# 56 unused floats between the activation buffers and the weight buffers of a hybrid encoder trunk

## The chip, the cores and the metric

The kernel runs on one core of one Trainium2 chip. The metric is the device time of one execution in microseconds (us), lower is better. Three timed runs of the kernel before gave 1882.45 us as median, from 1880.82 to 1882.71.

## The reference

Two layers of an encoder over 512 frames and 16 learned meta tokens, so 528 positions of width 1024. Every layer stands between two half-step SwiGLU feed-forward blocks. Layer 0 mixes with a gated convolution and a state space model, layer 1 with windowed attention; its second half keeps the 512 real positions only.

```
h = concatenate([meta, x])                      # 528 x 1024
for layer in range(2):
    h = h + 0.5 * (silu(n1(h) @ w_gate) * (n1(h) @ w_up)) @ w_down     # d_ff 2816
    mix = conv_ssm_mixer(nm(h)) if layer == 0 else window_attention(nm(h))
    h = h + mix                                 # layer 1: without the meta tokens
    h = h + 0.5 * (silu(n2(h) @ w_gate2) * (n2(h) @ w_up2)) @ w_down2
```

## The kernel before, in words

Everything is float32. TensorE multiplies in the float32r format, and to keep the precision each product is made of three: every weight block is split into a high part `wh` and a low part `wl`, every activation into `xh`, `xl` (or `act_h`, `act_l` behind the gate), and `mm3` (L790 to L801) adds wh*xh, wh*xl and wl*xh in PSUM.

The stationary operand (the one that LDWEIGHTS puts into the array) is a block of 128 columns of `wh` or `wl`; the moving operand is a row of an activation buffer, all positions of one group of 128 features. With 528 positions a row is streamed in two matmuls of 264 columns (`hf` 0 and 1, column description `ALL`), each with a weight load of its own; with 512 positions in one matmul of 512 (`FRONT`).

```
for q, (w, x) in enumerate(((wh, x_h), (wh, x_l), (wl, x_h))):
    for hf in range(nb):
        last = nc.tensor.matmul(ps[:, 2 * pair + hf, 0:nh], w[:, slot, b * P:(b + 1) * P],
                                x[:, k0 + k, c0 + hf * nh:c0 + (hf + 1) * nh], ...)
```

Feed-forward blocks 0 to 2 (`ffn`, through `x_job` and `mm3`, recorded at L799) run with 528 positions, block 3 with 512. L1015 is the input projection of layer 0, L1057 its output projection, L1076 keys and values of layer 1 (there the activations are stationary and the weights move), L1126 the queries, L1227 and L1265 the output projection of the attention.

**Where the operands lie.** Buffers stand one behind the other in each partition, in the order of their `sb` calls: `h`, `xh`, `xl`, `act_h`, `act_l`, `raw`, `wh`, `wl`, `t_a` and the smaller ones, `arena`. A row of the activations is padded from 528 to `ROW` = 576 floats, 2304 bytes, which is 9 times 256; a weight block is 512 bytes and all the large buffers are multiples of 256 bytes long. So an activation row and a weight block start at the same place modulo 256 (in the built program both at 128). From this follows the position of each moving operand relative to its stationary one, in bytes modulo 256:

- 528 positions: `hf` 0 at 0, `hf` 1 at 264 * 4 = 1056, which is +32
- 512 positions in block 3, L1227, L1265: 0 (in 48 of the 96 matmuls of L1265 the stationary operand, too, lies in the activation buffers, `w3h` and `w3l`)
- L1126 starts at position 16: +64
- L1076, where `xh` from position 16 on is stationary and the weights move: -64

The order of work is fixed. SP loads units of 16 weight blocks into the two slots of `raw` (`load_unit`, L699), each load waiting for the low part of an earlier unit (`wl_ready`); ScalarE copies `wh` from `raw` (L1276), VectorE subtracts to get `wl` (L1563), TensorE consumes the unit. ScalarE and VectorE also evaluate the gates, the norms and the residual (L1314 to L1316, L1599 to L1624) on tiles that `tile_full` announces.

Of the kernel before, what the change touches and what calls it, by code (L numbers as in the profile page):

```python
# [25 lines left out]
P = 128  # L26
# [6 lines left out]
def trunk_program(nc, a, out, stop=None):  # L33
# [56 lines left out]
    with ExitStack() as ctx:  # L90
        def sb(name, shape, dt=F32):
            return ctx.enter_context(nc.sbuf_tensor(name, shape, dt))
# [6 lines left out]
        xl = sb("xl", [P, KD, ROW], F32R)[:, :, 0:L]  # L99
        act_h = sb("act_h", [P, PART[0], ROW], F32R)[:, :, 0:L]  # L100
        act_l = sb("act_l", [P, PART[0], ROW], F32R)[:, :, 0:L]
        raw = sb("raw", [P, 2, UNITW])
        wh = sb("wh", [P, 2, UNITW], F32R)
        wl = sb("wl", [P, 2, UNITW], F32R)
# [1986 lines left out]
```

## Time and profile before

| | |
|---|---|
| timed, median of 3 | 1882.45 us |
| profiled execution, device time | 1882.0 us |
| its span, first to last instruction | 1880.0 us |
| TensorE matmuls / weight loads | 13887 / 13887 |
| granted TensorE clock, mean | 0.998 |

The profile gives for every engine its busy time, in groups of instructions by line, operation and operands. `PE` is a matmul, `PEld` a weight load. A matmul is pipelined: its duration in the trace runs from its start to the arrival of its last result, and the next one starts long before. What a matmul costs in a dense stretch is therefore the distance from one start to the next, which the timeline and the chain of work give, not the mean duration. The chain of work lists what the last instruction depended on, back to the beginning.

### The profile page before, as it was taken

The numbers are of one execution on the slowest core, as the hardware profiler recorded it, in microseconds if no ns is written. First come the engines' busy times: TensorE is split into PE (matmuls) and PEld (weight loads), VectorE is DVE, ScalarE is ACT, GpSimd is POOL, SyncE is SP. The second block draws the span as 40 slices with busy tenths as digits, with TensorE's granted clock in tenths as the row PEclk, the third lists the DMA queues.
The fourth block names the chain that finished last, engine by engine and source line by source line (L and its number), as shares of the span: only waits on it lengthen the run. The fifth ranks groups of instructions, "written<-read, shape, count | busy, mean of one in ns | idle before, by whom it ended". The sixth has DMA issues, their size and how long they took to land.

```text
span 1880.0 us, 33855 instructions
## 1 busy us (share of the span) xinstructions
PE 1865.3 (99%) x13887; PEld 1765.6 (94%) x13887; DVE 955.1 (51%) x1077; ACT 599.6 (32%) x707; POOL 350.8 (19%) x629
## 2 busy tenths in 40 slices
PE   8999999999999999999999999999999999999999
PEld 8999999999999999999999999999988788888887
DVE  5444356568765443344564443445556654434443
ACT  5222222332243222222342222223456442222232
POOL 2888889414330000000000000000012000000000
PEclk9999999999999999999999999999999999999999
DMA  7332444547523332433243323322321233333423
GB/s 183 90 84 84 142 147 128 163 126 185 137 69 90 90 84 84 120 82 83 70 126 90 84 84 101 90 81 71 112 73 46 62 96 92 92 94 104 110 70 87
DMA packets 330785, 188.29 MB, mean 100 GB/s; under 512 B 8152, under 2 KB 323832, under 8 KB 330712
## 3 DMA queue, kind: packets, MB, share of 16 engines
q1 hardware_dynamic: 323296, 166.81, 32.0%
q0 software_dynamic: 7088, 20.38, 4.0%
q8 instruction: 52, 0.85, 0.2%
q14 instruction: 21, 0.17, 0.0%
q10 hardware_dynamic: 328, 0.07, 0.0%
HBM read 174.91 MB, written 11.14 MB: 99 GB/s over the span
## 4 chain that ended last, share of the span: by engine, by line
PE 95%; DVE 2%; issue 1%; ACT 1%; DMA 1%; ACTq 0%; POOL 0%; SPq 0%; DVEq 0%
PE ps L799 78%; PE ps L1015 5%; PE ps L1057 2%; PE ps L1126 2%; PE ps L1076 1%; PE ps L1265 1%; PE ps L1227 1%; DMA raw<-in_ff_w_down 1%; PE ps L844 1%; PE ps L1167 0%; PE ps L976 0%; PE ps L975 0%; PE ps L966 0%; DVE r L1592 0%; DVE wl L1563 0%
## 5 line engine op out<-in xcount | busy, mean ns | idle before, releaser
L799 PE MATMUL ps<-xh,wh 128*128 128x264 f32 (+1 forms) x2432 | 557.7, 299 | 0.3 <-DVE t_a L1616 0.2
L799 PE MATMUL ps<-xh,wl 128*128 128x264 f32 (+1 forms) x2432 | 556.6, 298 | 0.0
L799 PE MATMUL ps<-xl,wh 128*128 128x264 f32 (+1 forms) x2432 | 556.6, 298 | 0.0
L1563 DVE TENSOR_TENSOR wl<-raw,wh 128x2048 fp32r<-128x2048 f32 x171 | 398.3, 2329 | 173.6 <-ACT wh L1276 173.6
L1276 ACT ACTIVATE wh<-raw 128x2048 fp32r<-128x2048 f32 x172 | 327.5, 1904 | 248.6 <-PE ps L799 205.7
L799 PEld LDWEIGHTS ps<-xh,wh 128*128 128x128 f32 x2432 | 384.9, 188 | 15.3 <-issue 1.4
L799 PEld LDWEIGHTS ps<-xl,wh 128*128 128x128 f32 x2432 | 384.8, 188 | 13.8 <-issue 0.2
L799 PEld LDWEIGHTS ps<-xh,wl 128*128 128x128 f32 x2432 | 384.8, 188 | 13.8
L799 PE MATMUL ps<-act_h,wh 128*128 128x264 f32 (+1 forms) x1232 | 282.2, 298 | 1.2 <-DVE wl L1563 1.2
L799 PE MATMUL ps<-act_h,wl 128*128 128x264 f32 (+1 forms) x1232 | 281.6, 298 | 0.0
L799 PE MATMUL ps<-act_l,wh 128*128 128x264 f32 (+1 forms) x1232 | 281.5, 298 | 0.0
L1619 DVE TENSOR_TENSOR t_c<-ps,r 128x528 f32<-128x528 f32 (+1 forms) x88 | 61.9, 704 | 358.3 <-PE ps L799 356.5
L799 PEld LDWEIGHTS ps<-act_h,wh 128*128 128x128 f32 x1232 | 194.8, 188 | 8.2 <-issue 1.4
L799 PEld LDWEIGHTS ps<-act_h,wl 128*128 128x128 f32 x1232 | 194.8, 188 | 7.0
L799 PEld LDWEIGHTS ps<-act_l,wh 128*128 128x128 f32 x1232 | 194.9, 188 | 6.6
L1316 ACT ACTIVATE act_h<-t_c 128x528 f32 (+3 forms) x88 | 56.5, 642 | 447.8 <-DVE t_c L1622 447.8
L326 POOL TENSOR_TENSOR arena<-arena 128x32 f32<-128x32 f32 (+6 forms) x253 | 183.1, 724 | 19.6
L676 POOL TENSOR_SCALAR arena<-arena 128x16 f32<-128x16 f32 x4 | 1.0, 258 | 871.6 <-DVE arena L1948 842.3
L1314 ACT ACTIVATE t_bs<-t_a 128x528 f32<-128x528 f32 (+1 forms) x88 | 56.5, 643 | 274.6 <-DVE t_a L1616 274.6
L1599 DVE SCALAR_TENSOR_TENSOR h<-ps,h 128x528 f32 (+2 forms) x72 | 50.6, 703 | 182.0 <-PE ps L799 174.9
L1624 DVE TENSOR_TENSOR act_l<-t_c,act_h 128x528 f32 (+3 forms) x88 | 65.8, 747 | 78.5 <-ACT act_h L1316 78.5
L1622 DVE TENSOR_TENSOR t_c<-t_c,t_bs 128x528 f32<-128x528 f32 (+1 forms) x88 | 68.0, 773 | 9.0
(308 smaller groups left out, 1681.3 us busy)
## 6 DMA issues: line engine op xcount, KB each, us to landing
raw<-in_ff_w_gate SPq DMA_DIRECT2D x88, 512.0 KB, 4.0
raw<-in_ff_w_up SPq DMA_DIRECT2D x87, 512.0 KB, 5.2
raw<-in_ff_w_down SPq DMA_DIRECT2D x64, 384.0 KB, 4.0
raw<-in_ff_w_down SPq DMA_DIRECT2D x64, 320.0 KB, 3.7
raw<-in_even_w_in SPq DMA_DIRECT2D x16, 512.0 KB, 5.3
raw<-in_attn_w_qkv SPq DMA_DIRECT2D x12, 512.0 KB, 4.4
raw<-in_even_w_out SPq DMA_DIRECT2D x8, 512.0 KB, 4.5
raw<-in_attn_w_o SPq DMA_DIRECT2D x8, 512.0 KB, 4.6
```

Source lines behind the costliest of these rows:

```text
L326: did(g.tensor_tensor(o, x, y, op))
L799: last = nc.tensor.matmul(ps[:, 2 * pair + hf, 0:nh], w[:, slot, b * P:(b + 1) * P], x[:, k0 + k, c0 + hf * nh:c0 + (hf + 1) * nh], start= ...
L1015: last = nc.tensor.matmul(ps[:, 2 * (p % 2) + hf, 0:L // 2], w[:, slot, b * P:(b + 1) * P], x[:, k, hf * L // 2:(hf + 1) * L // 2], start= ...
L1057: last = nc.tensor.matmul(ps[:, 2 * (d % 2) + hf, 0:L // 2], w[:, slot, b * P:(b + 1) * P], x[:, k, hf * L // 2:(hf + 1) * L // 2], start= ...
L1276: nc.scalar.activation(wh[:, c % 2, :], raw[:, c % 2, :], ACT.Copy).then_inc(wh_ready, 1)
L1314: nc.scalar.activation(t_b[:, cols], t_a[:, cols], ACT.Silu).then_inc(silu_done[n], 1)
L1316: nc.scalar.activation(act_h[:, s + 2 * i, span(operand(col))], t_c[:, cols], ACT.Copy).then_inc(act_h_done[n], 1)
L1563: v.tensor_tensor(wl[:, c % 2, :], raw[:, c % 2, :], wh[:, c % 2, :].bitcast(F32), ALU.subtract).then_inc(wl_ready, 1)
L1599: v.scalar_tensor_tensor(hd, tile(pair, col), scale, hd, ALU.mult, ALU.add).then_inc(tile_evac, 1)
L1619: v.tensor_tensor(halves(t_c, col), tile(1, col), halves(r, col), ALU.mult).then_inc(tile_evac, 1)
L1622: v.tensor_tensor(t_c[:, cols], t_c[:, cols], t_b[:, cols], ALU.mult).then_inc(gated[n], 1)
L1624: v.tensor_tensor(act_l[:, s + 2 * i, span(operand(col))], t_c[:, cols], act_h[:, s + 2 * i, span(operand(col))].bitcast(F32), ALU.subtrac ...
```

## The change

One buffer of 56 floats (224 bytes) per partition is allocated between `act_l` and `raw`. Nothing reads or writes it. `raw`, `wh`, `wl` and everything allocated after them move up by 224 bytes; `h`, `xh`, `xl`, `act_h`, `act_l` stay. No instruction is added, removed or reordered.

```
         act_h = sb("act_h", [P, PART[0], ROW], F32R)[:, :, 0:L]
         act_l = sb("act_l", [P, PART[0], ROW], F32R)[:, :, 0:L]
+        weight_pad = sb("weight_pad", [P, 56])
         raw = sb("raw", [P, 2, UNITW])
         wh = sb("wh", [P, 2, UNITW], F32R)
         wl = sb("wl", [P, 2, UNITW], F32R)
```

Relative to its stationary operand, modulo 256 bytes, each moving operand goes 32 bytes up: 528 positions from 0 and +32 to +32 and +64; 512 positions from 0 to +32; L1126 from +64 to +96; L1076, where the weights move, from -64 to -96. The 48 matmuls of L1265 with both operands in the activation buffers stay at 0.

## Rows read from the trace of the kernel before

**Rows 1.** The page: busy time of the engines, and granted clock in 40 slices

```profile
PE 1865.3 (99%) x13887; PEld 1765.6 (94%) x13887; DVE 955.1 (51%) x1077; ACT 599.6 (32%) x707; POOL 350.8 (19%) x629
...
PEclk9999999999999999999999999999999999999999
```

**Rows 2.** The chain of work, pieces in order: start us, us, what

```profile
43.73 299.54 PE ps L799 x2496
...
593.92 374.64 PE ps L799 x3120
...
975.25 368.88 PE ps L799 x3072
...
1523.87 307.64 PE ps L799 x1356
```

**Rows 3.** Waits of TensorE: waited for, us in total, times, longest

```profile
PE ps L916 <- DMA arena<-in_meta_tokens: 3.0, 1, 3.0
...
PE ps L799 <- DVE wl L1563: 1.2, 1, 1.2
```

**Rows 4.** Waits of the SP queue

```profile
SPq L703 <- DVE wl L1563: 1515.4, 167, 21.7
```

**Rows 5.** Groups by line and shape on TensorE: xcount, busy us, mean ns

```profile
L799 PE MATMUL ps<-xh,wh 128*128 128x264 f32 x2080 | 420.3, 283 | 0.1
...
L799 PE MATMUL ps<-act_h,wh 128*128 128x264 f32 x1056 | 213.1, 283 | 1.2 <-DVE wl L1563 1.2
...
L799 PE MATMUL ps<-xh,wh 128*128 128x512 f32 x352 | 137.5, 391 | 0.2 <-DVE t_a L1616 0.2
...
L799 PE MATMUL ps<-act_h,wh 128*128 128x512 f32 x176 | 69.1, 393 | 0.0
...
L1015 PE MATMUL ps<-xh,wh 128*128 128x264 f32 x256 | 53.3, 290 | 0.5 <-DVE arena L1751 0.5
...
L1126 PE MATMUL ps<-xh,wh 128*128 128x512 f32 x64 | 26.6, 415 | 0.0
L1057 PE MATMUL ps<-act_h,wh 128*128 128x264 f32 x128 | 25.8, 284 | 0.3 <-DVE act_l L1854 0.3
...
L1227 PE MATMUL ps<-act_h,wh 128*128 128x512 f32 x32 | 14.0, 436 | 0.0
L1076 PE MATMUL ps<-wh,xh 128*128 128x512 f32 x32 | 12.9, 402 | 0.0
...
L1265 PE MATMUL ps<-act_h,wh 128*128 128x512 f32 x16 | 6.2, 389 | 0.0
```

**Rows 6.** Weight loads of L799, the same columns

```profile
L799 PEld LDWEIGHTS ps<-xh,wh 128*128 128x128 f32 x2432 | 384.9, 188 | 15.3 <-issue 1.4
```

**Rows 7.** Timeline of TensorE in the first matmuls: start us, us, what

```profile
17.77 0.65 PE L844 MATMUL ps<-xh,wh 128*128 128x264 f32 x2
...
20.41 0.65 PE L844 MATMUL ps<-xh,wh 128*128 128x264 f32 x2
```

**Rows 8.** Timeline of TensorE in block 3, two matmuls, thirty-nine apart

```profile
1700.11 0.39 PE L799 MATMUL ps<-act_h,wh 128*128 128x512 f32 x1
...
1708.95 0.39 PE L799 MATMUL ps<-xh,wh 128*128 128x512 f32 x1
```

**Rows 9.** Timeline of TensorE in the queries, L1126, thirty-nine matmuls apart

```profile
1371.23 0.39 PE L1126 MATMUL ps<-xh,wh 128*128 128x512 f32 x1
...
1380.16 0.39 PE L1126 MATMUL ps<-xh,wh 128*128 128x512 f32 x1
```

**Rows 10.** Timeline of TensorE in keys and values, L1076, forty matmuls apart

```profile
1360.05 0.39 PE L1076 MATMUL ps<-wh,xh 128*128 128x512 f32 x1
...
1369.38 0.39 PE L1076 MATMUL ps<-wh,xl 128*128 128x512 f32 x1
```

**Rows 11.** Windows: busy (instructions) of PE, PEld, DVE, ACT, POOL; clock, DMA share, GB/s

```profile
0.00:40.00 40.00, 33.28 (x224) 32.28 (x225) 22.43 (x31) 23.40 (x35) 10.25 (x22) 0.91 0.77 197
40.00:400.00 360.00, 358.77 (x2989) 358.41 (x2988) 176.97 (x153) 101.35 (x91) 263.16 (x422) 1.00 0.41 119
...
550.00:1345.00 795.00, 794.93 (x6612) 794.14 (x6611) 369.20 (x342) 233.59 (x215) 6.81 (x13) 1.00 0.32 90
```

More of the change, by code:

```diff
@@ L101, in trunk_program @@
         act_l = sb("act_l", [P, PART[0], ROW], F32R)[:, :, 0:L]
+        weight_pad = sb("weight_pad", [P, 56])
         raw = sb("raw", [P, 2, UNITW])
```

## The prediction

> **What bounds the kernel now.** I read the page first. TensorE is busy for 99% of the span and has as many weight loads as matmuls; VectorE and ScalarE are half idle or more, and the clock is full in all forty slices [rows 1]. A busy TensorE can still be a waiting one, so the waits come next: the longest of TensorE is 3.0 us for the first input, and all waits for a weight unit in L799 together are 1.2 us [rows 3]. SP, which loads the weights, is ahead: it stands for 1515 us waiting for a slot to come free [rows 4]. The chain of work says the same: long pieces in which nothing but matmul follows matmul [rows 2]. So the time is the number of matmuls times the distance between two starts, and that distance is the only thing that an unused buffer can move.
>
> The distances. With 264 columns: 374.64 us for 3120 matmuls is 120.1 ns, 299.54 for 2496 is 120.0, 368.88 for 3072 is 120.1 [rows 2]. At 2.4 GHz and one column a cycle the columns alone are 110.0 ns, so 10.0 ns are on top. With 512 columns in block 3: from 1700.11 to 1708.95 are 39 matmuls, 226.7 ns each [rows 8]; columns alone 213.3, on top 13.3. In the first matmuls, at the low clock, 12 matmuls take 2.64 us, 220.0 ns each [rows 7], and 264 columns at 1.2 GHz are 220.0: nothing on top. So the extra belongs to the full clock and is no fixed price of an instruction. Every matmul has the load of the next weights beside it, which the trace shows with 188 ns from start to end whatever the matmul's length [rows 6]. A disturbance between the stream and the weight load is a reading that fits.
>
> The trace has the same matmul of 512 columns at two other relative positions. L1126 (+64): 1371.23 to 1380.16 for 39, 229.0 ns [rows 9]. L1076 (-64): 1360.05 to 1369.38 for 40, 233.3 ns [rows 10]. At 0 it was 226.7. So these positions come with up to 6.6 ns more, in stretches where no wait stands between the matmuls. That the position is the cause is an inference; L1076 also has the roles of the operands exchanged.
>
> **The change part by part.** Instructions, waits, DMAs and their order stay. What changes is the position of each moving operand against its weights, 32 bytes up.
>
> (a) 528 positions. The matmuls of 264 columns are three times those of the `wh` by high-part groups: (2080 + 1056 + 256 + 128) * 3 = 10560, or 5280 pairs [rows 5]; the few of L844, L859 and L1029 are left out. Today a pair is one at 0 and one at +32, 240.0 ns together. Afterwards it is one at +32 and one at +64. Whatever +32 costs stays in the pair; a 0 is exchanged for a +64. The only price for that exchange is the one from the 512-column rows, 229.0 - 226.7 = 2.3 ns. Sum: 5280 * 2.3 = +12.1 us.
>
> (b) 512 positions from 0 to +32: (352 + 176 + 32 + 16) * 3 = 1728 matmuls [rows 5]. No row shows a stretch of only +32. The bounds are the costs of its neighbours, 0 at one end and +2.3 at the other, and an inference below gives -6.7. I take the middle of the neighbours, 1.15 ns: +2.0 us.
>
> (c) L1126 from +64 to +96, 192 matmuls, and L1076 from -64 to -96, 96 matmuls [rows 5]. Both arrive between the two measured 229.0 and 233.3, so I take 231.1: 192 * 2.1 = +0.4 us and 96 * -2.2 = -0.2 us. The ends are 4.3 ns on 288 matmuls, 1.2 us.
>
> (d) The landings of the weights, and the operands of VectorE and ScalarE, move too. The DMAs are busy for 0.32 to 0.41 of the time in the long stretches [rows 11] and hidden by SP's lead [rows 4]; ScalarE and VectorE have 50% and more of slack [rows 1]. The exception is the first 40 us, with a DMA share of 0.77 [rows 11], where a slower landing would be seen; the landing place is no multiple of 256 bytes before or after, so I put it at 0 within 1 us. If a transfer did lose that cover everywhere, it would be seen as waits for `wl`, which are 1.2 us now.
>
> Nothing hides (a) to (c): where matmul follows matmul, each ns per matmul is a ns of the end. Sum: 12.1 + 2.0 + 0.4 - 0.2 = +14.3 us on the 1882.0 us of the profiled execution (span 1880.0, 2.0 around it): 1896.3. The median of the runs is 0.45 above that execution, so 1897.
>
> **A rule against the trace.** The distance from start to start has been worked out above from rows. The Trainium skill, "TensorE: Matmul & The Clock Gate", section "Step-by-step: what each phase is for", says that the moving operand and the weight load have read ports of their own, and that loading the next weights doesn't steal bandwidth from the running matmul. By that rule positions can't matter and the sum is 0, 1882.45. Rows 8 to 10 don't agree easily, as three distances stand for one shape. The same page, section "Back-to-back issue gap", puts 2.5 ns on top of the columns at full clock. The trace has 10.0 and 13.3; an estimate from that page for a placement free of any disturbance is 7.5 * 10560 + 10.8 * 1728 = 98 us less.
>
> **The rivals.**
>
> *Faster: +32 is the good place.* The weight load is the same under 264 and 512 columns [rows 6]. If the cost on top comes from it alone, it doesn't depend on the matmul's length: 13.3 ns at 0, and since a pair has 20.0 on top, 6.7 at +32. Then (b) gains 6.6 * 1728 = 11.4 us. The pair changes from 13.3 + 6.7 to 6.7 + x, with x the cost at +64. With L1126's x = 15.6 it loses 2.3 ns, 12.1 us, and all is even again. With x = 13.3 the pair stays at 240 and the result is 1871; with x = 6.7, if the good region reaches to +64, it gains 6.6 ns a pair, 34.8 us, together 46 us: 1836. It becomes faster by over 3.8 us when x is below about 14.8 ns. For it: the low cost of pairs, and that 264 columns may meet +64 otherwise than 512 do. Against it: 512 columns have time on top even after the load has long ended, so length may matter by itself, and then nothing says that +32 is better than 0.
>
> *No change.* Either the position doesn't matter, and L1126 and L1076 are slow for reasons of their own (their x starts 64 bytes into a row, their roles are exchanged), or gain and loss cancel as above. For it: 120.0 to 120.1 in three stretches hundreds of us apart [rows 2], as if the pair were held to a fixed step that a small shift needn't break. Time 1880 to 1886.
>
> *Much slower.* The new places cost what -64 costs, 6.6 ns more than 0: 5280 * 6.6 + 1728 * 6.6 = 46 us, 1929. For it: one of the three measured places is that dear, and the shift of the plain fp32 operands is not in any row.
>
> **How the numbers follow.** Slower in the moderate way, 1888 to 1910: 0.40; much slower, above that: 0.11; no change within 0.2% (3.8 us, which is about what a measurement of this kernel can tell): 0.16; faster: 0.33, most of it between 1836 and 1876. The likeliest is 1897, with 1888 to 1910 as its own range. As both signs hold much of the chance, the range must reach into both: 1845 leaves out the far part of the gain (0.09), 1925 the far part of the loss (0.08). The bound on that side from the rows, that all that is on top goes as in the stretch at low clock, would be 10.0 * 10560 + 13.3 * 1728 = 129 us; no matmul at full clock comes near it, and it stays outside.
>
> **What the profile after would show.** The chain's pieces give the distance again: 264 columns at 121.2 ns if (a) is right, 120.0 if nothing changed, under 119.6 if the pair gained. The timeline of block 3: 226.7 to 229.0 for (b), 220.0 in the first rival. L1126 and L1076 near 231. The waits of TensorE and the DMA share as before; if waits for `wl` have grown, (d) is wrong. The forecast falls if the pair at +32 and +64 doesn't follow the 512-column price of +64, on which 12 of the 14 us rest.

## The result and the profile after

The changed kernel takes 1895.85 us (median of 4 runs, 1895.63 to 1900.16) against 1882.3 before: a ratio of 1.0079, 95% interval 1.0061 to 1.0096. The profiled execution has a span of 1893.8 us where the one before had 1880.0, so 13.8 us are to be found.

The page of the changed kernel, busy time and clock:

```profile
PE 1879.3 (99%) x13887; PEld 1768.1 (93%) x13887; DVE 957.6 (51%) x1077; ACT 599.6 (32%) x707; POOL 349.4 (18%) x629
...
PEclk9999999999999999999999999999999999999999
```

The counts of instructions and the row of the clock are those of [rows 1]; TensorE is busy for 14.0 us more, its weight loads for 2.5. The waits of TensorE and of SP on the weights, and two windows with the DMA share as the last column but one:

```profile
PE ps L917 <- DMA arena<-in_meta_tokens: 3.2, 1, 3.2
...
PE ps L800 <- DVE wl L1564: 1.0, 1, 1.0
```

```profile
SPq L704 <- DVE wl L1564: 1530.3, 167, 21.9
```

```profile
0.00:40.00 40.00, 33.04 (x227) 32.13 (x228) 22.38 (x31) 23.46 (x35) 10.24 (x22) 0.91 0.80 201
40.00:400.00 360.00, 358.96 (x2970) 358.60 (x2970) 178.41 (x152) 100.38 (x91) 261.80 (x422) 1.00 0.40 118
```

These waits of TensorE have moved by 0.2 us or less [rows 3]. SP waits 14.9 us longer for free slots [rows 4], about as much as TensorE takes longer, so its lead is intact. The share of busy DMAs is 0.80 where it was 0.77 in the first 40 us and 0.40 where it was 0.41 after them [rows 11]. The first long piece of the chain even begins 0.3 us earlier. The loss lies in the matmuls themselves. The chain of work of the changed kernel (start us, us, what), every line number one up:

```profile
43.42 301.62 PE ps L800 x2496
...
596.52 374.67 PE ps L800 x3120
...
972.08 374.70 PE ps L800 x3120
...
1346.78 5.62 PE ps L1077 x24
...
1527.85 316.64 PE ps L800 x1356
```

Beside [rows 2]: block 0 takes 301.62 us for the same 2496 matmuls that took 299.54, 120.8 ns each where it was 120.0. Blocks 1 and 2 take 374.67 us for 3120, 120.1 ns, as before. Block 3 takes 316.64 us for the 1356 that took 307.64, which is 233.5 ns in place of 226.9 (the 226.7 ns of [rows 8] are thirty-nine of them; these are all 1356). By the starts of these pieces 2.9 us have come together at the beginning of block 1. The keys and values of layer 1 begin at 1346.78; in the chain of the kernel before they begin here:

```profile
1344.13 5.58 PE ps L1076 x24
```

So the loss is still 2.7 us there, and the remaining 11.1 of the 13.8 us arise behind it, where the long pieces have matmuls of 512 columns.

The clearest lines are in L1266 (L1265 before), where 48 matmuls with both operands in the activation buffers are followed by 48 with the weights in `wh` and `wl`. Timeline of the changed kernel:

```profile
1493.49 0.39 PE L1266 MATMUL ps<-act_h 128*128 128x512 f32 x1
...
1504.15 0.40 PE L1266 MATMUL ps<-act_h,act_l 128*128 128x512 f32 x1
1504.38 0.39 PE L1266 MATMUL ps<-act_h,wh 128*128 128x512 f32 x1
...
1515.35 0.40 PE L1266 MATMUL ps<-act_h,wl 128*128 128x512 f32 x1
```

47 distances in 10.66 us, 226.8 ns, while the relative position is the old 0; then 47 in 10.97 us, 233.4 ns, from the first weight block that the change has moved. Line and shape are the same, and the two stretches follow one another directly. The second 48 in the kernel before, at position 0:

```profile
1500.80 0.39 PE L1265 MATMUL ps<-act_h,wh 128*128 128x512 f32 x1
...
1511.45 0.39 PE L1265 MATMUL ps<-act_h,wl 128*128 128x512 f32 x1
```

47 distances in 10.65 us, 226.6 ns: before the change the two halves of this line ran alike. Queries (L1127, now at +96) and keys (L1077, now at -96):

```profile
1373.29 0.40 PE L1127 MATMUL ps<-xh,wh 128*128 128x512 f32 x1
...
1382.40 0.39 PE L1127 MATMUL ps<-xh,wh 128*128 128x512 f32 x1
```

```profile
1366.27 0.39 PE L1077 MATMUL ps<-wh,xh 128*128 128x512 f32 x1
...
1371.89 0.39 PE L1077 MATMUL ps<-wh,xh 128*128 128x512 f32 x1
```

39 distances of 233.6 ns (229.0 in [rows 9]) and 24 of 234.2 (233.3 in [rows 10]).

In the first matmuls, where the granted clock is 0.50 (1.2 GHz), the move costs nothing. The changed kernel there, two matmuls to a row:

```profile
17.06 0.65 PE L845 MATMUL ps<-xh,wl 128*128 128x264 f32 x2
...
19.70 0.65 PE L845 MATMUL ps<-xh,wl 128*128 128x264 f32 x2
```

12 matmuls in 2.64 us, 220.0 ns each, as in [rows 7] before the change.

### The profile page after: what moved, and what is told of

Read it like the earlier page. It is cut to its first block, busy times and chain, and to the rows that moved or that the text cites. A ratio compares the mean times of both kernels' runs of the same rounds, so it can differ in the third digit from the quotient of the medians.

```text
span 1893.8 us, 33855 instructions
## 1 busy us (share of the span) xinstructions
PE 1879.3 (99%) x13887; PEld 1768.1 (93%) x13887; DVE 957.6 (51%) x1077; ACT 599.6 (32%) x707; POOL 349.4 (18%) x629
## 4 chain that ended last, share of the span: by engine, by line
PE 95%; DVE 2%; issue 1%; ACT 1%; DMA 1%; ACTq 0%; POOL 0%; SPq 0%; DVEq 0%
PE ps L800 78%; PE ps L1016 5%; PE ps L1058 2%; PE ps L1127 2%; PE ps L1077 1%; PE ps L1266 1%; PE ps L1228 1%; DMA raw<-in_ff_w_down 1%; PE ps L845 0%; PE ps L1168 0%; PE ps L976 0%; PE ps L977 0%; PE ps L967 0%; PE ps L1189 0%; DVE wl L1564 0%
## 5 line engine op out<-in xcount | busy, mean ns | idle before, releaser
L1283 ACT ACTIVATE t_bs<-h 128x528 f32 (+1 forms) x40 | 25.7, 643 | 144.2 <-DVE h L1600 125.9
```

## The experiments

The theory after the result was A: the distance between two starts depends on the position of the moving operand relative to the stationary one, modulo 256 bytes. A pair is here the two matmuls of 264 columns that stream one row, the first half at the position named first. Rivals: B, the weights' own place counts; C, the small buffers that moved too have a part; and, of the pairs, that +32 is a good place and 0 a bad one.

**Who is it relative to?** Four kernels.

```
+        first_pad = sb("first_pad", [P, 56])
         h = sb("h", [P, KD, L])
```

> The 56 floats stand in front of h, so every buffer moves by 224 bytes and moving and stationary operand keep their relative positions (0 and +32; 0 in block 3). Theory A, the relative position sets the distance: 1882 us, block 3 at 226.7 ns a matmul. Theory B, the place of the weights by itself modulo 256 does (in the change they went from 128 to 96): 1896 us as with the change, block 3 at 233.3 ns.

```
         wl = sb("wl", [P, 2, UNITW], F32R)
+        small_pad = sb("small_pad", [P, 56])
         t_a = sb("t_a", [P, L])
```

> The 56 floats stand between wl and t_a: only the working buffers of VectorE and ScalarE, the plain fp32 operands and the arena move. Theory A: nothing to see, 1882 us and 226.7 ns in block 3. Theory C, that the small buffers had a part in the loss: some of the 13.6 us comes back, 1885 to 1896.

```
+        weight_pad = sb("weight_pad", [P, 64])
         raw = sb("raw", [P, 2, UNITW])
```

> 64 floats, 256 bytes, in place of 56. Theory A with a period of 256 bytes (or a divisor): as before the change, 1882 us, 226.7 ns in block 3, pairs of 264 at 240.0 ns. If any unused buffer at this place costs, or the true period is longer: near 1896.

The first took 1881.32 us (ratio 1.0002, 0.9992 to 1.0011), the second 1881.12 (1.0000, 0.9990 to 1.0010), the third 1881.39 (0.9999, 0.9990 to 1.0009). Block 3 in the chain of the first, all buffers moved together:

```profile
1522.84 307.65 PE ps L800 x1356
```

The 226.9 ns of before to the digit, with the weights at the very place that they have in the changed kernel. B is out. So is C, by the second kernel, and a buffer of 64 floats costs nothing, by the third, so that moving the weights by 256 bytes is as not moving them. The fourth makes the position from the other side, without any buffer: block 3 alone reads its moving operand 8 floats further up.

```
-    x[:, k0 + k, c0 + hf * nh:c0 + (hf + 1) * nh],
+    x[:, k0 + k, c0 + 8 * (nb == 1) + hf * nh:c0 + 8 * (nb == 1) + (hf + 1) * nh],
```

> The kernel before, no buffer moved; only the moving operand of block 3 (L799, 512 columns) is read from column 8 in place of 0, 32 bytes further up (the first 8 positions are left out and 8 of the padding are used; sizes stay). Relative position +32 made from the other side. Theory A: block 3 goes from 226.7 to 233.3 ns a matmul, 1584 matmuls, +10.5 us, 1893; the pairs of 264 stay at 240.0. Theory B, the weights' own place: 1882.

It took 1891.04 us (1.0049, 1.0032 to 1.0066); its chain:

```profile
43.66 299.54 PE ps L799 x2496
...
1523.79 316.63 PE ps L799 x1356
```

The pairs are untouched, and block 3 has the 233.5 ns of the changed kernel, again to the digit. That is A, shown from both sides. The landing place of the weights is out too, as no buffer moved here. And since weights 224 bytes up and a moving operand 32 bytes up cost the same, the period of 256 bytes is seen a second time.

**Which places cost what?** The same unused buffer with 48, 32, 8 and 60 floats, which puts block 3 at +64, +128, -32 and +16, and the pairs at that place and 32 bytes above it.

> 48 floats: block 3 at +64, pairs at +64 and +96. If the distance depends on the relative position alone, block 3 takes what the queries took at +64 before the change, 229.0 ns: +2.3 * 1728 = +4 us; the pairs, one half further from the old place, 240 to 242 ns: 1886 to 1894. Theory D, that 0 is good and every other place is as dear as +32 (233.3 ns): 1893 or more.

> 32 floats: block 3 at +128, pairs at +128 and +160, half a period away. No row has it. Theory D: 233 ns, 1893 or more. If the distance goes up and down with the position (226.7 at 0, 233.3 at +32, 229.0 at +64, 233.3 at -64): 227 to 233 ns, 1882 to 1893. Under 226.7 ns in block 3 would be a place better than the old one.

> 8 floats: block 3 at -32, pairs at -32 and 0. If the sign of the distance doesn't matter, -32 is as dear as +32: 233.3 ns, +11 us from block 3, 1893, and the pairs stay near 240 ns, as their halves are still 32 bytes apart. If what counts is that one half of a pair stands at 0: exactly 240.0 ns in all stretches.

> 60 floats: block 3 at +16, pairs at +16 and +48. If the grain of the effect is 32 bytes, +16 behaves as 0 or as +32: 226.7 or 233.3 ns in block 3. If it is finer: something between, near 230 ns, 1888.

Their chains, in this order:

```profile
42.95 292.82 PE ps L800 x2400
594.86 386.68 PE ps L800 x3168
...
1545.15 310.65 PE ps L800 x1356
```

```profile
43.21 260.48 PE ps L800 x2112
599.13 387.38 PE ps L800 x3168
...
1551.04 316.63 PE ps L800 x1356
```

```profile
42.78 299.54 PE ps L800 x2496
593.11 374.65 PE ps L800 x3120
...
1525.25 316.65 PE ps L800 x1356
```

```profile
42.20 299.54 PE ps L800 x2496
592.20 374.64 PE ps L800 x3120
...
1523.10 307.65 PE ps L800 x1356
```

Divided out, with the kernels before and after beside them (for a pair the first and the second long piece; the ratio is the time against the kernel before, timed beside it):

| block 3 at | ns per 512 | pair at | ns per pair | time, us | ratio (95%) |
|---|---|---|---|---|---|
| 0 (before) | 226.9 | 0, +32 | 240.0 / 240.2 | 1882.3 | |
| +16 | 226.9 | +16, +48 | 240.0 / 240.2 | 1881.97 | 1.0001 (0.9992 to 1.0011) |
| +32 (the change) | 233.5 | +32, +64 | 241.7 / 240.2 | 1895.85 | 1.0079 (1.0061 to 1.0096) |
| +64 | 229.1 | +64, +96 | 244.0 / 244.1 | 1905.85 | 1.0129 (1.0112 to 1.0146) |
| +128 | 233.5 | +128, +160 | 246.7 / 244.6 | 1918.43 | 1.0195 (1.0178 to 1.0212) |
| -32 | 233.5 | -32, 0 | 240.0 / 240.2 | 1893.23 | 1.0060 (1.0043 to 1.0077) |

Block 3 at +64 has 229.1 ns, as expected, the distance that the queries had at +64 before the change, so the 229.0 ns of [rows 9] were a matter of the place. This also refutes theory D, by which +64 costs what +32 costs. The kernel with 32 floats brings L1077 from -64 to +64, with the weights as the moving operand. Twenty of its matmuls:

```profile
1369.22 0.39 PE L1077 MATMUL ps<-wl,xh 128*128 128x512 f32 x1
...
1373.80 0.39 PE L1077 MATMUL ps<-wh,xl 128*128 128x512 f32 x1
```

4.58 us, 229.0 ns: at +64 the role of the buffers doesn't matter. The queries add to the map. Forty-eight of them in the chain of the kernel before (+64) and of the kernels with 48, 32, 8 and 60 floats, where they stand at +128, -64, +32 and +80:

```profile
1370.01 11.00 PE ps L1126 x48
```

```profile
1389.12 11.20 PE ps L1127 x48
```

```profile
1394.44 11.20 PE ps L1127 x48
```

```profile
1369.23 11.20 PE ps L1127 x48
```

```profile
1368.30 11.00 PE ps L1127 x48
```

That is 229.2 ns at +64 and +80, and 233.3 ns at +128, -64 and +32. The queries' rows start 64 bytes into a row of the buffer in all five, so their 229.0 ns aren't a matter of that start. From 0 to +16 and from +64 to +80, 16 bytes change nothing.

My expectation for +64 and +128 as a whole was too low, by 12 and by 25 us, nearly all of it because of the pairs; block 3 at +128 has the cost of +32. (1.5 us of each profiled execution is the clock: behind the small matmuls of the attention, from 1404 and from 1409 us on, it was granted at 0.51 and 0.52 over 3 us, nearly all at the lower level of 1.2 GHz, and 24 queries took 7.25 us where the changed kernel, at full clock, took 5.70.) At -32 block 3 costs what +32 costs and the time is the expected 1893; the pairs keep their 240.0 ns. Of the places tried none was better than the old one, so no version beat both kernels.

**What is a pair's price made of?** In both kernels the second half of a row in `mm3` was read from column 256 in place of 264, which puts both halves at one position.

```
-    x[:, k0 + k, c0 + hf * nh:c0 + (hf + 1) * nh],
+    x[:, k0 + k, c0 + hf * 256:c0 + hf * 256 + nh],
```

> The changed kernel in which the second half of each row in mm3 is read from column 256 in place of 264 (so the last 8 positions are left out and 8 are used twice; number and size of the matmuls stay). Both halves then stand at +32. If the good price of the pairs before was that of +32 (my first rival), a pair takes about 233 ns and L1 to block 2 become 30 us shorter, near 1864. If +32 costs 264 columns what it costs 512 ones (6.6 ns more than 0), a pair is dearer than the 240 to 241.7 ns of the changed kernel, about 253, and the time near 1940. If pairs are held to 240 ns by something else, 1896.

> The kernel before in which the second half of each row in mm3 is read from column 256 in place of 264 (the last 8 positions are left out, 8 are used twice). Both halves stand at 0. If the cost on top belongs to the position alone, 13.3 ns at 0 as in block 3, a pair is 246.7 ns and the time 1882 + 31 = 1913. If 264 columns at 0 cost the 10.0 ns that the mean of a pair shows, 1882.

On the changed kernel (both at +32) 1916.04 us (1.0184, 1.0167 to 1.0201), on the kernel before (both at 0) 1912.16 (1.0163, 1.0146 to 1.0180). The long piece of block 1, of the first and of the second:

```profile
595.82 388.25 PE ps L800 x3168
```

```profile
597.98 390.83 PE ps L799 x3168
```

245.1 ns a pair at +32 and +32, 246.7 at 0 and 0. So one matmul of 264 columns costs 12.6 ns above its 110.0 at +32 and 13.4 at 0, and a pair at 0 and +32 would cost 245.9 ns if these added up. It costs 240.0. At 0 the cost on top is nearly the same for 264 and 512 columns, 13.4 and 13.5 ns, as my first rival had it; at +32 it is 12.6 and 20.2, and there the rival falls. The edit changes one thing besides the position: the second half no longer goes on where the first one ended. All pairs of the table do go on there, and they take from 240.0 to 246.7 ns, so that alone makes no pair cheap; halves 32 bytes apart that don't follow each other weren't run.

**Is the weight load the partner?** In block 3 only 64 of the 128 weight columns are loaded and used, in both kernels. This leaves out half of the outputs as well, so each matmul also writes 64 partitions of PSUM in place of 128.

```
-    last = nc.tensor.matmul(ps[:, 2 * pair + hf, 0:nh], w[:, slot, b * P:(b + 1) * P],
+    last = nc.tensor.matmul(ps[0:P if nb > 1 else 64, 2 * pair + hf, 0:nh], w[:, slot, b * P:b * P + (P if nb > 1 else 64)],
```

> The changed kernel; in block 3 only 64 of the 128 weight columns are loaded and used (half of the outputs are left out; the matmuls stream the same 512 columns). Theory A, in which the stream loses time while the next weights are read beside it: the 20.0 ns on top fall, to about half, 223 ns a matmul, 16 us less than the changed kernel. If the stream loses time for a reason of its own, independent of the load: 233.3 ns, no gain.

> The same with the kernel before: 64 of 128 weight columns in block 3. Theory A: the 13.3 ns on top fall to about half, 220 ns a matmul, 10 us less, 1872. Load without a part in it: 226.7 ns, 1882. Together with the same edit on the changed kernel: if the load is the partner, the difference between the two, 6.6 ns a matmul, shrinks as well.

A load is then 134 to 135 ns long in place of 188. One of its groups in the kernel before with short loads, between 1530 and 1830 us, and block 3 in the chain of that kernel and of the changed one with short loads:

```profile
L799 PEld LDWEIGHTS ps<-xh,wl 128*64 128x64 f32 x326 | 43.8, 134 | 30.5
```

```profile
1522.99 312.06 PE ps L799 x1356
```

```profile
590.74 383.04 PE ps L800 x3168
974.67 377.24 PE ps L800 x3120
...
1392.35 7.25 PE ps L1127 x24
...
1534.51 313.20 PE ps L800 x1356
```

The changed kernel falls from 233.5 to 231.0 ns, the kernel before rises from 226.9 to 230.1. What the position makes shrinks from 6.6 to 0.8 ns. That fits the weight load as the partner, but doesn't prove it, since the width of the output changed with it; what points at the load more strongly is that the place of the stationary operand counts at all, as the load is what reads it.

The simple form of A, in which half a load costs half, is refuted: at +32 the matmul should have come to 223 ns and came to 231.0, and at 0 it is dearer by 3.3 ns. The times are 1895.35 us (1.0065, 1.0046 to 1.0085) and 1885.85 (1.0024, 1.0015 to 1.0034). In the profiled execution of the former, 1898.58 us, the 3.4 us that block 3 gained are more than lost elsewhere: 1.5 us in 24 queries, at a granted clock of 0.52 as with +64 and +128 above, and 5 us in the pairs, whose code and positions are those of the changed kernel and whose second and third piece ran at 120.9 ns a matmul in place of 120.1. The same queries in the changed kernel, at full clock:

```profile
1387.23 5.70 PE ps L1127 x24
```

A pair at +32 and +64 has two steady distances, 240.2 and about 241.8 ns, and either can hold for hundreds of us. So one execution isn't enough to price this placement. The four timed runs with short loads lie between 1890.85 and 1898.58 us. Blocks 1 and 2 at the dearer distance would make 5 us, an estimate from these pieces; the slowest run of the changed kernel, 1900.16, is 4 us above the others, with a granted clock of 0.996 where they have 0.998. Only one execution of each was profiled, so how much of the spread is the pairs and how much the clock isn't shown.

## Why the prediction was right, and where it wasn't

The direction, the time (1897 against 1895.85) and the place of the bound were right: it is the distance between the starts of matmuls, and the relative position sets it. The sizes were not. The total is near by luck, because two terms were wrong in opposite directions: (a) +12.1 us forecast, 3.0 measured from the start of the first long piece to the keys; (b) +2.0 forecast, 10.5 measured; (c) +0.2 forecast, 0.7 measured from the keys to the output projection.

- That the time is the number of matmuls times the distance between starts, and that nothing hides it: right. The waits of TensorE shown moved by 0.2 us at most.
- That the relative position sets the distance, an inference from [rows 8 to 10]: right, and now shown by moving all buffers (no effect), the weights alone and the moving operand alone (the same effect).
- Step (a), a pair loses 2.3 ns because a half at 0 becomes a half at +64, +12.1 us: wrong in size. All that arose before the keys is 2.7 us, 3.0 with the earlier start: 1.7 ns a pair in block 0, nothing in blocks 1 and 2 (750.21 us before, 750.26 after). The step that failed is the transfer of a 512-column price to one half of a pair. The halves' costs don't add: at 0 and at +32 alone they are 13.4 and 12.6 ns, and 20.0 together.
- Step (b), 512 columns from 0 to +32 at the middle of the two neighbours, +1.15 ns: wrong in size. It is +6.6 ns, 10.5 us of the 11.1 that arose behind the keys; +32 is dearer than both neighbours. The other bound that I named, -6.7, had the size and the wrong sign. The sign that I gave for a failed forecast, the pair at +32 and +64 not following the price of +64, did occur.
- Step (c), between the two measured places, 231.1 ns: 233.6 and 234.2 measured; 192 * 4.6 + 96 * 0.9 ns is 1.0 us where 0.2 stood (0.7 by the chain).
- Step (d), landings and other operands at nothing: right, and moving the small buffers alone changed nothing. Two readings in the prediction were a little too round: VectorE, busy for 51%, has 49% of slack, and the nines of the clock row stand for 90% or more (0.91 in the first 40 us [rows 11]). Nothing hung on them.
- That the extra belongs to the full clock: right. At a granted clock of 0.50 the changed kernel has the same 220.0 ns.
- The rule of the Trainium skill, "TensorE: Matmul & The Clock Gate", section "Step-by-step: what each phase is for", by which loading the next weights doesn't steal read bandwidth from the running matmul, and the conclusion from it that positions can't matter: the runs disagree. With one and the same stream the distance went from 226.9 to 233.5 ns when only the place of the weights changed.
- The rival "+32 is the good place" is refuted by equal halves at +32, 245.1 ns a pair. "Much slower" had the right price for 512 columns and a wrong one for the pairs.

What stays open is the mechanism. A map of costs by position for 512 columns, 226.9 at 0 and +16, 229.1 at +64 (229.2 at +80 in the queries), 233.5 at +32, -32 and +128, is measured; why a shorter load is dearer at 0, and why halves 32 bytes apart are cheap near 0 and not at +64 and +96, isn't explained by anything run here. One observation may help whoever goes on: a load is 188 ns long in the trace and two starts of a pair are 120.0 ns apart, so by the trace a load lies beside both halves, where with 512 columns it lies beside one matmul. Whether that makes the joint price of a pair wasn't tested.

## What to carry to other kernels

In a kernel like this one, in which float32r matmul follows float32r matmul with a weight load each, the addresses of the two operands are a parameter of the schedule: an unused buffer of 128 bytes cost 2%, one of 256 bytes nothing. Other formats weren't run. Read the distance from start to start in each stretch, not the busy share, compare it with the columns at the granted clock, and try offsets in steps of 32 bytes, for each matmul shape on its own, since a place can be dear for one shape and not for another: at -32 the 512 columns lost 6.6 ns and the pairs nothing. And a few measured points of such a map must not be joined by a straight line: the forecast did that, and only the sum came out right, by luck.

## What the runs showed that was not expected

- At the low clock there is nothing on top of the columns (220.0 ns for 264, [rows 7], and the same at +32 and +64); at the full clock 264 columns take 120.0 to 123.4 ns and 512 take 226.6 to 234.2.
- Two matmuls of 264 columns, one at 0 and one at +32, take 240.0 ns together, less than twice either alone (246.7 and 245.1).
- A stream of 512 columns beside a load of 64 weight columns, with 64 output columns, (230.1 ns) is slower than beside one of 128 (226.9), at position 0.
- The same pairs at the same positions, +32 and +64, ran steadily at 240.2 ns in blocks 1 and 2 of one execution and at 241.8 in those of another.
